# One inference step of a two-layer hybrid diffusion backbone: attention in groups of score maps with two score buffers, differential maps combined before they are transposed, convolution taps inside the input projection, the convolution's norm ahead of attention, one barrier per layer

## The reference

```python
h = _rms(x, p['norm1_g']) * (1.0 + sc1) + sh1
u = h @ p['w_in']                       # 2048 columns, split among four mixers
...
o_a = _gqa_attend(qa, ka_all, va_all)   # 4 query heads, 2 key heads, 64 wide
o_b = _multiscale_pool(pool_in, ...)
o_c = _conformer_conv(glu_in, ...)      # 31 taps per channel, channel norm, silu, 256x256 product
# differential attention, 4 heads, two maps of 32 columns each:
p = jax.nn.softmax(s1, axis=-1) - lam * jax.nn.softmax(s2, axis=-1)
o_d = jnp.einsum('bhqk,bkhd->bqhd', p, v)
out = jnp.concatenate([o_a, o_b, o_c, o_d], axis=-1) @ p['w_out']
x = x + g1 * out
x = x + g2 * _expert_choice_ffn(h2, ...)  # 16 experts, 80 rows each
```

## Time and profile before

| what | value |
|---|---|
| median of 3 runs | 2094.1 us (2091.14 to 2098.71) |
| profiled execution, its own time | 2095.24 us |
| profiled execution, span of its trace | 2093.4 us |
| TensorE busy | 1795.2 us (86% of the span) |
| VectorE, ScalarE, GpSimd busy | 541.1, 499.1, 353.5 us |
| moved by DMA | 533.86 MB, mean 255 GB/s |
| mean granted TensorE clock | 0.924 of full speed |

### The profile page before, as it was taken

The page is one execution under the profiler, slowest core; times in us unless marked ns, Lnnn a source line. Parts: engine busy times, 40 slices in busy tenths (PEclk is TensorE's granted clock), DMA queues, the critical chain, the costliest instruction groups (busy, mean ns, idle before and its releaser), DMA issues.

```text
span 2093.4 us, 66619 instructions
## 1 busy us (share of the span) xinstructions
PE 1795.2 (86%) x30560; PEld 1438.4 (69%) x30560; DVE 541.1 (26%) x961; ACT 499.1 (24%) x1268; POOL 353.5 (17%) x320
## 2 busy tenths in 40 slices
PE   3998887984999999899959998889569999998994
PEld 2554665453898889888835556645369988898894
DVE  2130785324011110101114157723500101111011
ACT  2011563211122121211211135521121221212122
POOL 1130765000000000000003156600000000000001
PEclk8999997996999999999979999989679999999997
DMA  9200600529899999999960060032479999999995
GB/s 392 90 1 10 240 2 16 226 91 354 317 394 395 391 399 388 400 390 394 396 236 0 1 243 8 2 115 97 181 290 384 394 394 393 396 390 399 389 393 210
DMA packets 136654, 533.86 MB, mean 255 GB/s; under 512 B 5889, under 2 KB 6977, under 8 KB 136321
## 3 DMA queue, kind: packets, MB, share of 16 engines
q1 hardware_dynamic: 121616, 482.53, 58.6%
q0 software_dynamic: 6336, 21.63, 4.3%
q10 hardware_dynamic: 8624, 28.61, 3.6%
HBM read 508.33 MB, written 24.41 MB: 254 GB/s over the span
## 4 chain that ended last, share of the span: by engine, by line
PE 51%; DMA 35%; DVE 6%; ACT 4%; issue 3%; POOL 1%; POOLq 0%; ACTq 0%; DVEq 0%; SPq 0%; PEldq 0%; PEld 0%
DMA ring<-in_exp_w_down 18%; PE PS L655 18%; DMA ring<-in_exp_w_up 11%; PE PS L542 6%; PE PS L439 4%; PE PS L403 3%; PE PS L404 3%; PE PS L487 3%; PE PS L475 2%; PE PS L504 2%; DMA arena<-xn_rows,arena 2%; DMA x_rows<-arena 2%; PE PS L405 2%; DMA ring<-in_w_mod 2%; PE PS L351 1%
## 5 line engine op out<-in xcount | busy, mean ns | idle before, releaser
L655 PE MATMUL PS<-arena,ring 128*64 128x80 f32 x24576 | 919.3, 237 | 90.7 <-DMA ring<-in_exp_w_up 44.0
L655 PEld LDWEIGHTS PS<-arena,ring 128*64 128x64 f32 x24576 | 906.9, 140 | 105.9 <-issue 105.5
L922 ACT ACTIVATE arena<-PS,modB,modA 128x64 f32<-128x64 f32 (+1 forms) x544 | 153.5, 422 | 377.9 <-PE PS L642 377.9
L1428 POOL DMA_INDIRECT x_rows<-arena x32 | 45.7, 1429 | 752.1 <-DVE arena L1280 752.1
L542 PE MATMUL PS<-ring,H 128*128 128x512 f32 x320 | 139.2, 593 | 1.7 <-ACTq L700 1.7
L1267 DVE TENSOR_TENSOR arena<-arena,PS 128x320 f32<-128x320 f32 x64 | 31.4, 490 | 322.6 <-PE PS L655 322.6
L542 PEld LDWEIGHTS PS<-ring,H 128*128 128x128 f32 x320 | 60.0, 190 | 73.8 <-issue 71.7
L439 PE MATMUL PS<-H,ring 128*128 128x512 f32 x192 | 102.4, 616 | 6.2 <-DVE arena L1038 4.6
L1314 POOL TENSOR_SCALAR stat<-stat 128x1 f32<-128x1 f32 (+2 forms) x45 | 17.7, 394 | 519.4 <-ACT arena L883 213.4
L1146 DVE SCALAR_TENSOR_TENSOR arena<-arena,par 128x655 f32<-128x655 f32 x82 | 101.7, 1241 | 1.2
L935 ACT ACTIVATE arena<-PS 128x320 f32<-128x320 f32 x32 | 14.0, 439 | 347.5 <-PE PS L655 347.5
(11 more groups left out here) (182 smaller groups left out, 1611.5 us busy)
## 6 DMA issues: line engine op xcount, KB each, us to landing
ring<-in_exp_w_gate SPq DMA_DIRECT2D x64, 2048.0 KB, 19.2
ring<-in_exp_w_up SPq DMA_DIRECT2D x64, 2048.0 KB, 18.2
ring<-in_exp_w_down SPq DMA_DIRECT2D x64, 2048.0 KB, 19.1
ring<-in_w_mod SPq DMA_DIRECT2D x24, 2048.0 KB, 15.6
ring<-in_w_in SPq DMA_DIRECT2D x8, 2048.0 KB, 24.0
ring<-in_w_out SPq DMA_DIRECT2D x4, 2048.0 KB, 18.2
arena<-x_rows ACTq DMA_DIRECT2D x15, 512.0 KB, 6.8
x_rows<-arena ACTq DMA_DIRECT2D x10, 512.0 KB, 2.6
```

The source lines that it names most:

```text
L655: last = mm(PS[r0:r0 + HD, b0 + j // 4, (j % 4) * CAP:(j % 4 + 1) * CAP], ring[:, 2 * m + k // 4, k % 4, j * P + r0:j * P + r0 + HD], movi ...
L922: last = do(xeT[:, jj, c0:c1], PS[:, 6 + part, j * CAP + c0:j * CAP + c1], ACT.Identity, bias=modB[:, 1, v, jj:jj + 1], scale=modA[:, 1, v ...
```

## The change

- **Attention** goes by 27 groups: six per latent tile (four differential groups `d` with the two maps of a head, two GQA groups `g` with two maps) and three groups of four small maps for the context tile, placed after tile 0. Two score buffers of three banks alternate, so the scores of a group wait for the exponentials of the group but one before. One DVE instruction takes the maxima of both maps. `combine` adds the second map of a differential head, scaled by minus lambda times the ratio of the sums, onto the first, and only the result is turned and multiplied with the values: eight jobs per latent tile where there were 12. The turned chunks go by fours (`FILLS`, 42 per layer) through one bank, `T_BANK`; five buffers hold the copies.
- **Taps.** DVE does 52 taps and POOL 10, all inside the input projection, at the places `("c", n)` and `("k", n)` of `TAKE_ORDER`; the pooling means are there too (`p`). The `f` steps of the convolution come ahead of the `j` steps in layer 0 and in the middle of them in layer 1.
- **Modulation product 2** is made inside the projection (`m`), and each `j` step behind it waits until DVE has copied it out (`mod_taken`).
- **The convolution's norm** and products 3 and 4 stand between projection and attention; the whole output projection of tile 0 stands behind attention.
- **Barriers** 1 to 3 of each layer are gone; semaphores on the single results stand in their place.
- The slots of modulation products 3, 4, 5 and of layer 1's product 0 in the ring are exchanged, and the load of product 4 stands ahead of that of `w_out`.

```diff
-        POOL_TAPS = 19
+        POOL_TAPS = 10
         DVE_TAPS = TAPS - POOL_TAPS
...
+        GROUPS = [(kind, t, i) for t in (0,) for kind, i in TILE] + [("c", LT, 0), ("c", LT, 1), ("c", LT, 2)] \
+            + [(kind, t, i) for t in (1, 2, 3) for kind, i in TILE]
...
+                    if ("m", 2) in ORDER[l][:ORDER[l].index(("j", t))]:
+                        pe.wait_ge(mod_taken, MODS_DONE[l, 2])
...
+                def scores(l, g):
+                    kind, t, i = GROUPS[g]
+                    if g >= 2:
+                        pe.wait_ge(t_exp, NEXP * l + EXPS[g - 2])
...
+                def turn_probs(l, f):
+                    pe.wait_ge(t_pt, NF * l + f)
...
+                    for g in range(NG + 1):
+                        if g + 1 < NG:
+                            scores(l, g + 1)
+                        for f in GROUP_FILLS[g - 1] if g else ():
+                            turn_probs(l, f)
+                            long = 0
+                            while waiting and CHUNKS[waiting[0]][-1][0] < f and long < LT + 1:
+                                long += len(CHUNKS[waiting[0]])
+                                values(l, waiting.pop(0))
...
+                turn_mod(l, 4, mix_rows[2], 3, 1)
+                pe.wait_ge(pooled, 2 * l + 1)
                 mix_pools(0)
...
+                pe.wait_ge(pooled, 2 * l + 2)
+                pe.wait_ge(mods_ready, 2 * l + 2)
...
                 for kind, n in TAKE_ORDER[l]:
-                    if kind == "x":
+                    if kind == "c":
+                        for _ in range(n):
+                            conv_tap(*taps.pop(0))
+                    elif kind == "m":
+                        take_mod(l, 2, mix_rows[0], MOD2_BANK[l])
+                    elif kind == "x":
...
+                    for a in range(n):
+                        first, second = probs_at(g, 2 * a), probs_at(g, 2 * a + 1)
+                        last = V.scalar_tensor_tensor(first, second, ratio[:, a:a + 1], first, ALU.mult, ALU.add)
+                    last.then_inc(t_comb, 1)
...
+ORDER = ((("x", 0), ("x", 1), ("x", 2), ("x", 3), ("x", 4), ("f", 0), ("f", 2), ("f", 3), ("f", 4), ("f", 5), ("m", 2),
+          ("j", 0), ("j", 1), ("q", 0), ("j", 2), ("q", 1), ("j", 3), ("q", 2), ("j", 4), ("q", 3), ("f", 1), ("q", 4)),
+         (("x", 0), ("x", 1), ("j", 0), ("x", 2), ("j", 1), ("q", 0), ("x", 3), ("x", 4), ("f", 2), ("f", 3), ("q", 1),
+          ("f", 4), ("f", 5), ("m", 2), ("j", 2), ("f", 0), ("j", 3), ("q", 2), ("j", 4), ("q", 3), ("f", 1), ("q", 4)))
...
+               ("p", 0), ("f", 2), ("f", 3), ("c", 5), ("f", 4), ("f", 5), ("k", 5), ("c", 9), ("m", 2), ("j", 0),
+               ("c", 7), ("k", 1), ("q", 0), ("j", 1), ("c", 7), ("k", 1), ("q", 1), ("j", 2), ("c", 7), ("k", 1),
+               ("q", 2), ("j", 3), ("c", 7), ("k", 1), ("q", 3), ("j", 4), ("c", 5), ("k", 1), ("f", 1), ("p", 1),
+               ("c", 5), ("q", 4)),
...
+               ("z", 0), ("j", 1), ("f", 2), ("f", 3), ("c", 2), ("q", 1), ("c", 8), ("f", 4), ("f", 5), ("k", 4),
+               ("c", 14), ("m", 2), ("j", 2), ("c", 13), ("k", 3), ("f", 0), ("q", 2), ("j", 3), ("c", 7), ("k", 1),
+               ("q", 3), ("j", 4), ("k", 2), ("c", 6), ("f", 1), ("p", 0), ("p", 1), ("c", 2), ("q", 4)))
```

More of the change, by code:

```diff
@@ new lines, in backbone_step_kernel @@
+        EXPS, SLOT, n_exps, n_slots = [], [], 0, 0
+        for g, (kind, t, i) in enumerate(GROUPS):
+            SLOT.append(n_slots)
+            n_slots += 1 if kind == "c" else 2
+            n_exps += 4 if kind == "c" else 2
+            EXPS.append(n_exps)
+        NEXP = n_exps
+        SHARED = [sum(2 if x[0] == "c" else 1 for x in GROUPS[:g + 1]) for g in range(NG)]
+        N_SHARED = SHARED[-1]
+        COMBS = {g: n for n, g in enumerate(g for g, x in enumerate(GROUPS)
+                                            if x[0] == "d" or x[0] == "c" and x[2] > 0)}
@@ new lines, in probs_at, with slot_freed @@
+        def probs_at(g, a):
+            if GROUPS[g][0] == "c":
+                return Pm[:, SLOT[g] % 5, a * P:(a + 1) * P]
+            return Pm[:, (SLOT[g] + a) % 5, :]
+        def slot_freed(k):
+            fills, combs = 0, 0
+            for j, (g, a, gqa, h) in enumerate(JOBS):
+                if k == SLOT[g] + (0 if GROUPS[g][0] == "c" else a):
+                    fills = max(fills, CHUNKS[j][-1][0] + 1)
+                if not gqa and GROUPS[g][0] == "d" and k == SLOT[g] + 1:
+                    combs = COMBS[g] + 1
+            return fills, combs
@@ L503, in values @@
                         for half in (0, HD):
[L504 to L506 removed]
+                            last = mm(O_BANK[half:half + HD, o0:o0 + HD],
+                                      PT[:, f % 5, i * P + half:i * P + half + HD], v,
+                                      start=(c == 0), stop=(c == len(CHUNKS[j]) - 1))
@@ L534, in _ @@
[L534 to L546 removed]
+                    turned_out[0] = n + 1
@@ new lines, in attention @@
+                def attention(l):
+                    waiting = list(range(NJ))
+                    scores(l, 0)
+                    for g in range(NG + 1):
[7 more added lines that the diff above has]
+                                values(l, waiting.pop(0))
+                        for t in TILES:
+                            if LAST_GROUP[t] + 5 == g:
+                                pe.wait_ge(t_pt, NF * l + GROUP_FILLS[g - 1][-1] + 1)
+                                turn_out(l, t)
+                    while waiting:
+                        values(l, waiting.pop(0))
@@ L585, in _, with project_out @@
                     last.then_inc(c_pw, 1)
-                finish_phase(l, 3)
+                attention(l)
+                def project_out(l, t):
+                    if t >= 2:
+                        pe.wait_ge(o_g, NT * l + t - 1)
+                    pe.wait_ge(t_oTe, NT * l + TILES.index(t) + 1)
+                    for k in (0, 1, 6, 7, 2, 3, 4, 5):
+                        for c in range(2):
+                            last = mm(PS[:, 2 * (t % 2) + c, :], H[:, k, t * P:(t + 1) * P],
+                                      ring[:, wout + k // 4, k % 4, c * 512:(c + 1) * 512],
+                                      start=(k == 0), stop=(k == 5))
+                    last.then_inc(o_mm, 1)
                 def norm2_turn(l, t):
@@ new lines, in _ @@
+                wait_apart(act, state_saved, 64 * (l + 1))
+                for g in range(STEPS):
+                    if g == NG:
+                        wait_apart(act, gates_saved, 32 * l + 16)
+                        for v in range(2):
+                            act.dma_start(gb1[:, v, :], modg[l, 0, v:v + 1, :].to_broadcast([P, D]))\
+                               .then_inc(g_loaded, 16)
+                        for t in range(2):
+                            act.dma_start(xo[:, t, :], x_rows(l, t)).then_inc(xo_loaded[t], 16)
+                    maps = list(range(len(group_maps(g)))) if g < NG else []
+                    fills = list(GROUP_FILLS[g - 1]) if 1 <= g <= NG else []
+                    if fills and GROUPS[g - 1][0] == "g":
+                        while maps or fills:
+                            if maps:
+                                exponentials(l, g, maps.pop(0))
+                            if fills:
+                                take_probs(l, fills.pop(0))
+                    for a in maps:
+                        exponentials(l, g, a)
+                    for f in fills:
+                        take_probs(l, f)
+                    for t in TILES:
+                        if LAST_GROUP[t] + 5 == g:
+                            take_out(l, t)
@@ L1101, in _ @@
                         step_f(l, n)
-                finish_phase(l, 1)
+                assert not taps
+                dve.wait_ge(taps_done, l + 1)
+                V.tensor_tensor(y3[:, 1, :], y3[:, 1, :], tapsum, ALU.add).then_inc(c_y, 1)
                 dve.wait_ge(lam_exps, l + 1)
```

597 lines of the change are left out of this document (295 added, 302 removed), and 6 rows, old and new, of the table TAKE_ORDER.

## The result

| | kernel before | changed kernel |
|---|---|---|
| median | 2096.4 us (4 runs) | 2156.2 us (2150.5 to 2162.3, 4 runs) |
| profiled execution, its own time | 2095.2 us | 2159.2 us |
| span | 2093.4 us | 2157.1 us |
| ratio to before | | 1.029 (95% interval 1.027 to 1.031) |

The account below looks back on a forecast made before the run. PE was taken as the bound (51% of the span, DMA 35%). Layer 0's terms summed to -25.1 us and layer 1's to -6.7, 31.8 less than 2095.2: 2063 us, forecast 2045 to 2080 (chance 0.50), range 2034 to 2093.

Parts of the forecast that it names:

- the first one: Whole kernel: DMA's 35% of the chain is expert weights, untouched; only the stretch ahead of each layer's experts can move.
- DMA's share in the experts: Experts of both layers, a sign to check in the changed profile: this share should stay as it is.
- rival A: Attention: turned chunks through one bank starve PE and lower its clock; tiles 29 to 30 us, total 2117; chance 0.15.
- The norm: Convolution norm between projection and attention: 28 and 33 us against 32.1, so -4.1 in layer 0, +0.9 in layer 1.
- The projection: Input projection: +9.9 us in layer 0 and +23.3 in layer 1, with waits at product 2 of 10.8 and 16.0.
- rival B: Projection and attention: shorter waits at product 2 (5.9 and 11.2), attention 104 us per layer; total about 2040; chance 0.17.
- Attention: Attention in each layer: 112.7 us against 149.6, 36.9 less, with latent tiles at 23.3 us.
- The output projection: Output projection after attention: the half hidden under the reciprocal now lies open, 7.0 us more per layer.
- Rival C: Input projection: a DVE tap and a POOL tap instruction cannot overlap; nine taps 25.4 us, total 2092; chance 0.18.

Follow-up runs that it names:

- 64: Changed kernel with 64 empty TensorE instructions ahead of layer 1's expert loop: 2071.3 us, ratio to before 0.988.
- 180: Kernel before with 180 empty TensorE instructions ahead of layer 1's expert loop: 2184.4 us, ratio 1.040.
- 94: Changed kernel with 94 empty TensorE instructions ahead of layer 0's expert loop, none ahead of layer 1's: 2153.4 us.
- 20: Changed kernel with 20 empty TensorE instructions ahead of layer 1's expert loop: 2153.3 us.
- 30: Changed kernel with 30 empty TensorE instructions ahead of layer 1's expert loop: 2073.4 us.
- the run with both orders: Changed kernel with 64 empty instructions; VectorE copies product 2 before its taps and does the end taps ahead of the second gate: 2026.9 us, ratio 0.968.
- product 2 first: Changed kernel with 64 empty instructions; VectorE copies product 2 ahead of nine taps in layer 0 and 14 in layer 1: 2044.6 us.
- the two runs with the turns first: Changed kernel with 64 empty instructions, turns and values ahead of scores: 2271.8 us with one score buffer's order, 2256.7 us with both buffers kept.

## Why the prediction was wrong

**The step that failed** is the first one: "The DMA part is the experts' weights, which the change does not touch; what can move is the stretch ahead of each layer's experts." The change takes 744 matmuls and as many weight loads out of TensorE's program (30560 of each on the page of before, 29816 on that of after), none of them in the loops, and so moved a loop that it doesn't touch over a border. (By these alone the first border in layer 1's loop would have gone from 204 to 156, still in seven sections; other instructions that were put in ahead of it, which no view counts, did the rest to 24.) That is +84.4 in layer 1, shown by removing it (64), by giving it to the kernel before (180), by moving it to layer 0 (94), and by its border (20 and 30). The last of the prediction's signs, DMA's share in the experts, which was to stay, shows it: 0.87 for 0.98. None of the rivals had it: rival A alone was on the slow side, by another mechanism. With the loop put back, the changed kernel takes 2071.3, 8 us above the forecast and inside its range.

**The norm** was the other term that failed, by 15 us over the two layers. "DVE reaches the add late: behind `j4` come five taps in layer 0 (3 us late)": there were ten, in two groups of five, at 1.49 each beside GpSimd's pooling means, and the add was 11.5 late; layer 1's eight took 12.3, and it was 9.2 late for 8. The rest of the excess, some 3 us a layer, lies behind the add: from its start to the first scores pass 28.3 and 28.7 us, for the 25 of the sum. What makes them is open. The late taps don't: in the run with both orders the same stretch takes 29.8 and 30.2.

**The projection** came out as worked out: waits of 9.7 and 15.6 for 10.8 and 16.0, nine taps 11.6 us for 12.9, stretches +7.5 and +26.0 for +9.9 and +23.3. Layer 1's excess is in TensorE's busy time: 7.8 us more, where 3.7 for product 2 and 2 for a restart were reckoned, at a clock of 0.92 for 0.97. Two small sums of the prediction are off, without weight: the parts ahead of `j0` add up to 14.3, not 14.5, and rival B's wait in layer 1 to 10.4, not 11.2. That the waits were a real cost, and not just VectorE's lack of time seen early, was left open in the prediction; product 2 first shows it (26.7 us).

**Attention** was right in its sum, -38.3 and -38.5 for -36.9, but not in its parts. Here is layer 0's: the start, tile 0 and the context tile; tile 1; tile 2; tile 3; the end.

```profile
254.40:287.10 32.70, 29.15 (x289) 19.96 (x288) 15.91 (x21) 20.85 (x54) 0.00 (x0) 0.79 0.13 52
287.10:313.80 26.70, 23.67 (x214) 16.12 (x210) 19.32 (x37) 14.08 (x37) 2.44 (x4) 0.74 0.01 2
313.80:335.30 21.50, 20.12 (x261) 14.38 (x260) 15.78 (x25) 15.96 (x36) 1.20 (x2) 1.00 0.01 2
335.30:357.00 21.70, 20.32 (x256) 14.35 (x252) 15.64 (x26) 15.51 (x37) 1.20 (x2) 1.00 0.01 2
357.00:365.70 8.70, 6.84 (x120) 5.25 (x116) 2.07 (x4) 5.06 (x11) 0.00 (x0) 1.00 0.40 126
```

A tile at full clock takes 21.5 where 23.3 was forecast. The start, tile 0 and the context tile take 32.7 for 38.8 (6.5 + 23.3 + 9), in spite of a clock of 0.79; tile 1 takes 3.4 more than forecast, with 2.3 us of waits for combinations and a clock of 0.74; tile 3 with the end takes 30.4 for 27.3. That these errors cancel to 1.4 us is luck; that each tile got shorter is not. Rival A (a single bank for turned chunks starves TensorE) falls: tile 2 has one wait of 0.69 for ACT's copy and runs at 1.00. That something of its kind is near shows in the two runs with the turns first, where TensorE waits 26 and 25 times in 27 groups and the whole attention runs at 0.58 and 0.62. The output projection, +7.5 and +4.8 for +7.0, was right.

**Rival C** (a tap on VectorE and one on GpSimd can't overlap) falls: nine taps took 11.6 us, not 25.4, while GpSimd was busy with five instructions of its own, 9.7 us. The rule of the Trainium skill that was set beside it (SBUF — State Buffer, "Who interferes with whom") would have these stand one after the other; the run without GpSimd's taps shows a slowdown by a third, 0.97 to 1.27 us, and no lockout of a whole instruction.

## What to carry to other kernels

A long loop (here some 1580 instructions: held in seven sections, loaded again in eight) is sensitive to where it starts: after any edit ahead of it, compare its time, its "issue" waits and the instruction queue's packets with those of before, and if they grew, shift it by some tens of empty instructions where the engine waits anyway. Where an engine waits for another that is behind, ask where that other one was idle earlier: moving its work there gave 44 us here with no instruction added. And a change that is judged by its total alone, 60 us slower here, may hold a gain (70 us, once the loop is shifted and the taps stand elsewhere).

## What the runs showed of the hardware

- TensorE's program is loaded in sections of 256 instructions, one packet of some 16.4 KB each. A loop of some 1580 in seven sections runs freely (4 to 5 us of "issue" waits in 16 passes, nearly all in the first). With 21 or 41 of them in an eighth, six or seven of the 16 passes are loaded again, each for nine packets and some 12 to 13 us; where it was seven, the loop took 83 to 89 us more. With 13 in the eighth the stalls ended after the third pass. Why 13 differs from 21, and why the passes between are spared, was not tried.
- An empty instruction that raises a semaphore costs TensorE about 0.15 us (248 took 37.8 us), so a shift should be small or stand under a wait: 64 are some 10 us, under the 16.1.
